# Folding the last square of each norm's sum into TensorE, and five reordered steps, in a two-block network on one core

## The chip, the core and the metric

The kernel runs on one core of a Trainium2 chip. A core has a matrix engine (TensorE, PE in the profile, with its weight loads as PEld), VectorE (DVE), ScalarE (ACT), GpSimd (POOL) and SyncE (SP), which here only starts transfers. The engines run their own instruction lists in order and meet only through semaphores. The metric is the device time of one execution in microseconds. Three executions of the kernel before took 1575.3, 1575.3 and 1575.46 us, median 1575.3.

## What is computed

Two network blocks follow one another on 512 tokens of 1024 features, everything in float32. In short:

```python
# first block
shift, scale, gate = split(silu(c) @ ada_w[0] + ada_b[0], 3)
h = rmsnorm(x, norm_g[0]) * (1 + scale) + shift
x = x + gate * mamba2_mixer(h)      # in-projection, conv, chunked state space scan,
                                    # y * silu(z), rms over each of 4 groups of 512, out-projection
kv = (rmsnorm(x, kv_norm_g) * (1 + kv_scale) + kv_shift) @ kv_w
x = x + gate1 * stick_breaking_mixer(rmsnorm(x, norm_g[1]) * (1 + scale1) + shift1, kv)
x = rmsnorm(x, final_g)
# second block
z = rmsnorm(x, norm_mix_g) @ w_in          # then an HGRN2 mixer and a banded attention
x = x + merged @ w_out
h2 = rmsnorm(x, norm_ffn_g); x = x + (silu(h2 @ w_gate) * (h2 @ w_up)) @ w_down
x = x + sigmoid(rmsnorm(x, norm_ple_g) @ w_ple_gate) * (p @ w_ple_proj)
```

Each `rmsnorm` needs the mean of the squares over the 1024 features of a token (over 512 in the mamba mixer's groups). The features lie on partitions, in 8 (or 4) tiles of 128, so the sum of squares is a sum over tiles and then over partitions.

## The kernel before

**Layout.** `X[:, k, :]` holds feature tile k of the residual stream for all 512 tokens. A projection is a row of output blocks of 128 features, each accumulated in one of three PSUM banks over the feature tiles k. float32 is reached by splitting: ScalarE rounds an operand to a high part, VectorE subtracts it to get the low part, and TensorE adds three products in the reduced float format (L646 high x high, L647, L648). The weights come in chunks of 128 x 2048 words through two buffers: SyncE loads `raw`, ScalarE makes `whi` (L1857, function `high`), VectorE makes `wlo` (L1162, function `rest`). The helper `behind(kind, n)` puts one such conversion, that of the chunk after the one of block (kind, n), at the place in an engine's list where it is called.

**Order.** There is no scheduler. Each engine's list is written by hand in one function, and `weave` mixes two or three generators by fixed counts of steps: where a generator yields decides what stands between its pieces on that engine. `Once` leaves out waits that an earlier one already covers.

**Sums of squares.** ScalarE squares tile after tile into `SQ` or one of three `T` tiles (L1877). An adder sums them in `SQ` (or `R`): VectorE for the first norm (L1183), GpSimd for all others (L2430). When the last add is done (`s_sqa`), TensorE multiplies the 128 x 128 matrix `ones` by that tile as true float32 (L690, function `sum_of`), which leaves the sum over partitions in all partitions of a bank. ScalarE turns it into 1/sqrt in `R` (L1864, L1865). There are ten such sums: `x`, `y0` to `y3` (four squares each), `out`, two for `so` (accumulated in `R` and `SQ`), `wo` and `fd`.

**The places around the change.**
- Start: `sum_of("x")` stands after the second of eight groups of small matmuls that make the first `ada` vector; ScalarE's copies for those groups (L1917) stand behind its 1/sqrt.
- After block cv 1 of the in-projection, VectorE copies the two transposed `dt` tables out of PSUM (L1349, L1350), and TensorE uses them (L789) four feature steps later.
- The scan (`ssd`): unit u = 4g + c is chunk c of group g, written in four pieces. On VectorE piece 2 ends with the state update (L1311, L1316), piece 3 makes `XD` and `XW` (L1321, L1327) and, for c = 0, the four gated products of the previous group (L1333). On TensorE `sum_of` of the previous group stands at the head of piece 2 of c = 2. The last group's pieces are woven into the out-projection (`out_proj`, a piece every two or three of its steps).
- kv: TensorE first makes the eight blocks `pp` of an unrelated product (L824 to L826), with `sum_of("out")` among them. ScalarE copies each to `PO` (L2084) and makes the eight high parts of the kv input (L1890); VectorE makes `T` (L1112) and the low parts (L1116). Then come the kv projections, the first two blocks together (`both`: 8 feature steps of 6 matmuls).
- sb: the same pattern once more for the query projection, whose first two blocks stand behind the kv blocks.

## Time and profile before

| | |
|---|---|
| median of 3 executions | 1575.3 us |
| profiled execution, its own time | 1575.3 us |
| its span, first to last instruction | 1573.5 us |
| TensorE busy | 1539.8 us, 98% of the span |
| VectorE, ScalarE, GpSimd busy | 954.1, 678.2, 114.2 us |
| mean granted clock of TensorE | 0.992 |
| float32 sums over partitions (L690) | 20 records, two for each of 10 |
| GpSimd adds (L2430) | 47 |

Busy time of TensorE includes the tail of each pipelined matmul, so a gap shows as idle only beyond that tail. The number behind the arrow in brackets names what ended an idle stretch. The first 12.9 us of TensorE are a wait for the first weights. Rows of several engines in one fence below are in order of time.

### The profile page before, as it was taken

What the parts mean: (1) busy time and instruction counts of PE and PEld (TensorE: products, weight loads), DVE (VectorE), ACT (ScalarE), POOL (GpSimd) and SP (SyncE); (2) the same over time, 40 slices, a digit from 0 to 9 for tenths busy, and PEclk for the clock granted to TensorE, in tenths of its full rate; (3) what the DMA queues carried; (4) which work ended last, traced back from release to release, by engine and by line L of the source; (5) the groups of instructions that cost most, each with busy time, mean ns of one, the idle gap of its engine ahead of it and who ended that gap; (6) DMA issues with size and microseconds to landing.
All of it is one profiled execution on the core that took longest, in us unless ns stands there. A gap on an engine that the chain in (4) does not pass through costs nothing. (4 is left out here: it accounts for less than half of the span.)

```text
span 1573.5 us, 19600 instructions
## 1 busy us (share of the span) xinstructions
PE 1539.8 (98%) x7978; PEld 1230.4 (78%) x7978; DVE 954.1 (61%) x1201; ACT 678.2 (43%) x958; POOL 114.2 (7%) x78
## 2 busy tenths in 40 slices
PE   5999999989999999999999999999999999999998
PEld 3788887868889766678898886678888888888877
DVE  4769798997882756765358536654544444332445
ACT  4556576764432555654222355533342322231232
POOL 0000000123300000014000000000120000000110
PEclk7999999999999999999999999999999999999999
DMA  7434344424592210113211122122222222222233
GB/s 324 163 134 154 132 147 143 148 69 173 215 369 112 81 54 27 54 55 110 93 69 54 54 81 94 68 77 84 83 105 98 90 107 82 105 101 101 76 111 120
DMA packets 47384, 177.74 MB, mean 113 GB/s; under 512 B 3616, under 2 KB 20512, under 8 KB 31680
## 3 DMA queue, kind: packets, MB, share of 16 engines
q1 hardware_dynamic: 30368, 167.44, 28.6%
q10 hardware_dynamic: 16928, 9.06, 2.2%
q8 instruction: 63, 1.03, 0.3%
q14 instruction: 25, 0.20, 0.0%
HBM read 172.23 MB, written 4.26 MB: 112 GB/s over the span
## 5 line engine op out<-in xcount | busy, mean ns | idle before, releaser
L646 PE MATMUL bank<-HH,whi 128*128 128x512 f32 x1352 | 554.4, 410 | 2.0 <-issue 1.6
L648 PE MATMUL bank<-HH,wlo 128*128 128x512 f32 x1352 | 528.5, 391 | 0.0
L647 PE MATMUL bank<-HL,whi 128*128 128x512 f32 x1352 | 528.2, 391 | 0.0
L1162 DVE TENSOR_TENSOR wlo<-raw,whi 128x2048 fp32r<-128x2048 f32 (+2 forms) x118 | 267.4, 2266 | 111.7 <-ACT whi L1857 110.4
L646 PEld LDWEIGHTS bank<-HH,whi 128*128 128x128 f32 x1352 | 254.6, 188 | 79.3 <-issue 33.0
L648 PEld LDWEIGHTS bank<-HH,wlo 128*128 128x128 f32 x1352 | 254.4, 188 | 54.7
L647 PEld LDWEIGHTS bank<-HL,whi 128*128 128x128 f32 x1352 | 255.0, 189 | 47.8 <-issue 3.1
L1857 ACT ACTIVATE whi<-raw 128x2048 fp32r<-128x2048 f32 (+2 forms) x118 | 222.4, 1884 | 102.9 <-PE bank L648 102.8
L2430 POOL TENSOR_TENSOR SR<-SR,tmp 128x512 f32<-128x512 f32 x35 | 61.6, 1761 | 592.9 <-ACT tmp L1877 591.9
L678 PE MATMUL bank<-whi,HH 128*128 128x256 f32 x256 | 74.3, 290 | 0.0
L679 PE MATMUL bank<-whi,HL 128*128 128x256 f32 x256 | 72.4, 283 | 0.0
L680 PE MATMUL bank<-wlo,HH 128*128 128x256 f32 x256 | 72.4, 283 | 0.0
L1481 DVE TENSOR_TENSOR_SCAN W<-W,cc 128x511 f32<-128x511 f32 (+3 forms) x64 | 49.0, 808 | 34.6 <-ACT W L2163 34.5
L648 PE MATMUL bank<-FH,wlo 128*128 128x512 f32 x176 | 68.5, 389 | 0.0
L647 PE MATMUL bank<-FL,whi 128*128 128x512 f32 x176 | 68.5, 389 | 0.0
L646 PE MATMUL bank<-FH,whi 128*128 128x512 f32 x176 | 68.5, 389 | 0.0
L1788 DVE TENSOR_TENSOR pst<-bank,SR 128x512 f32<-128x512 f32 x22 | 15.1, 692 | 72.0 <-PE bank L648 72.0
L1800 DVE SCALAR_TENSOR_TENSOR tmp<-tmp,bank 128x512 f32<-128x512 f32 x22 | 15.1, 688 | 65.0 <-PE bank L648 65.0
L2399 ACT ACTIVATE FH<-tmp 128x512 fp32r<-128x512 f32 x22 | 13.9, 632 | 85.9 <-DVE tmp L1800 85.9
L679 PEld LDWEIGHTS bank<-whi,HL 128*128 128x128 f32 x256 | 49.1, 192 | 1.0 <-issue 1.0
L678 PEld LDWEIGHTS bank<-whi,HH 128*128 128x128 f32 x256 | 49.1, 192 | 1.0 <-issue 1.0
L2395 ACT ACTIVATE tmp<-pst 128x512 f32<-128x512 f32 x22 | 13.9, 632 | 82.4 <-DVE pst L1788 82.4
(310 smaller groups left out, 2139.9 us busy)
## 6 DMA issues: line engine op xcount, KB each, us to landing
raw<-wstream SPq DMA_DIRECT2D x113, 1024.0 KB, 4.8
aslot<-tstream SPq DMA_DIRECT2D x24, 512.0 KB, 3.3
A<-astream SPq DMA_DIRECT2D x8, 1024.0 KB, 18.3
AC<-scratch ACTq DMA_DIRECT2D x16, 512.0 KB, 5.2
QT<-tstream SPq DMA_DIRECT2D x12, 512.0 KB, 5.8
OZ<-tstream SPq DMA_DIRECT2D x12, 512.0 KB, 7.3
raw<-wstream SPq DMA_DIRECT2D x4, 768.0 KB, 4.3
X<-xT SPq DMA_DIRECT2D x1, 2048.0 KB, 8.3
```

The costliest lines, as they stand in the source:

```text
L646: e.matmul(o, wh[:, k, c], hi[:, kb0 + k, :], start=first and k == 0, stop=False)
L647: e.matmul(o, wh[:, k, c], lo[:, kb0 + k, :], start=False, stop=False)
L648: x = e.matmul(o, wl[:, k, c], hi[:, kb0 + k, :], start=False, stop=last and k == kb - 1)
L678: e.matmul(o, HH[:, k, ts], wh[:, k, :], start=(k == 0), stop=False)
L679: e.matmul(o, HL[:, k, ts], wh[:, k, :], start=False, stop=False)
L680: x = e.matmul(o, HH[:, k, ts], wl[:, k, :], start=False, stop=(k == 7))
L1162: e.tensor_tensor(wlo[:, i % 2, 0:n], raw[:, i % 2, 0:n], whi[:, i % 2, 0:n].bitcast(F32), ALU.subtract).then_inc(s_lo, 1)
L1481: x = e.tensor_tensor_scan(k, k, diag[:, last], 0.0, ALU.mult, ALU.add)
L1788: e.tensor_tensor(pstage[n % 3][:, :], bank_of("fg", n)[:, :], R, ALU.mult).then_inc(s_fgr, 1)
L1800: e.scalar_tensor_tensor(q, q, 0.5, bank_of("fu", n)[:, :], ALU.mult, ALU.mult).then_inc(s_fu, 1)
L1857: e.activation(whi[:, i % 2, 0:n], raw[:, i % 2, 0:n], ACT.Copy).then_inc(s_hi, 1)
L2430: e.tensor_tensor(acc, acc, tile, ALU.add).then_inc(s_sqa, 1)
```

## The change

- `sum_of` makes two float32 products with `ones` into the same bank: the accumulated tile, and the last square straight from its own tile. The last add of each sum goes away (one on VectorE, nine on GpSimd), so `s_sqa` counts less; the second product waits for `s_sq`.
- `sum_of` of y0 to y2 stands at the end of the scan's piece 1 on TensorE, not at the head of piece 2.
- VectorE's gated products (L1333) move from the end of the scan's piece 3 to the end of piece 2.
- VectorE's two copies of the `dt` tables come one step of the in-projection later.
- kv: `sum_of("out")` and its 1/sqrt come after two `pp` blocks, not four; ScalarE's eight high parts stand behind all eight copies to `PO`; the conversion of the second kv chunk stands behind the load of the sigmoid tables.
- sb: the conversion of the second query chunk comes after the fifth of eight feature tiles, on ScalarE (from after the seventh) and on VectorE (from after the eighth).

```diff
--- before.py
+++ after.py
@@ -186,7 +186,7 @@
 HH_AT, HL_AT = h_table()
 
 SQ_AT = {"x": 0, "y0": 8, "y1": 12, "y2": 16, "y3": 20, "out": 24, "so": 32, "wo": 48, "fd": 56}
-SA_AT = {"x": 0, "y0": 7, "y1": 10, "y2": 13, "y3": 16, "out": 19, "so": 26, "wo": 40, "fd": 47}
+SA_AT = {"x": 0, "y0": 6, "y1": 8, "y2": 10, "y3": 12, "out": 14, "so": 20, "wo": 32, "fd": 38}
 SUM_AT = {"x": 1, "y0": 2, "y1": 3, "y2": 4, "y3": 5, "out": 6, "so2": 7, "so": 8, "wo": 9, "fd": 10}
 
 
@@ -683,11 +683,13 @@
             if half == 1:
                 x.then_inc(s_blk, 1)
 
-        def sum_of(name, bank, acc=SQ, n=7):
+        def sum_of(name, bank, q, acc=SQ, sqa=None, sq=None):
 
             w.wait_ge(l_con, 16)
-            w.wait_ge(s_sqa, SA_AT[name] + n)
-            e.matmul(bank[:, :], ones, acc[:, :], start=True, stop=True).then_inc(s_sum, 1)
+            w.wait_ge(s_sqa, sqa or SA_AT[name] + {"y": 2}.get(name[0], 6))
+            e.matmul(bank[:, :], ones, acc[:, :], start=True, stop=False)
+            w.wait_ge(s_sq, sq or SQ_AT[name] + {"y": 4}.get(name[0], 8))
+            e.matmul(bank[:, :], ones, q, start=False, stop=True).then_inc(s_sum, 1)
 
 
         def fold(i):
@@ -708,7 +710,7 @@
                              A[i][:, 256 * k:256 * k + 256], start=(k < 4), stop=(k > 3))
             x.then_inc(s_mv, 1)
             if i == 1:
-                sum_of("x", aux[0])
+                sum_of("x", aux[0], T[0][:, :])
             if i > 0:
                 fold(i - 1)
         fold(7)
@@ -736,10 +738,10 @@
                         x = e.matmul(aux[3][:, 128 * q:128 * q + 128], flat(ST[:, 2 * q:2 * q + 2, :]),
                                      Cc[g % 2][:, 128 * c:128 * c + 128], start=True, stop=True)
                     x.then_inc(s_to, 1)
-                yield
                 if 0 < g < 4 and c == 2:
                     w.wait_ge(s_cb, min(g + 1, 4))
-                    sum_of(f"y{g - 1}", aux[1], n=3)
+                    sum_of(f"y{g - 1}", aux[1], R)
+                yield
                 if u < 15:
                     if cv_ == 0:
                         w.wait_ge(s_fin, 10 * gv + 1)
@@ -799,7 +801,7 @@
                 yield from blocks(chunk_of["out", 8 * g + n], [("out", 8 * g + n)], (n % 4,), 512,
                                   h_ready(f"out{g}"), HH, HL, 4 * (g % 2))
                 if g == 2 and n == 3:
-                    sum_of("y3", aux[1], n=3)
+                    sum_of("y3", aux[1], R)
                 yield
 
         weave((chain(out_proj(0), out_proj(1)), 66), (chunks, 28))
@@ -813,8 +815,8 @@
         i = chunk_of["pp", 0]
         wh, wl = (t[:, i % 2, :].rearrange("p (k n) -> p k n", k=2) for t in (whi, wlo))
         for n in range(8):
-            if n == 4:
-                sum_of("out", aux[0])
+            if n == 2:
+                sum_of("out", aux[0], T[0][:, :])
             o, c = aux[1 + n % 4][:, :], slice(128 * n, 128 * n + 128)
             w.wait_ge(s_hi, i + 1)
             w.wait_ge(s_lo, i + 1)
@@ -907,10 +909,10 @@
         first = both("hq", 0, "in2")
         run(take(first, 3))
         w.wait_ge(s_bk, 32)
-        sum_of("so", aux[1], R, 13)
+        sum_of("so", aux[1], T[0][:, :], R, SA_AT["so"] + 11, SQ_AT["so"] + 15)
         run(first)
         run(block("hq", 2, "in2"))
-        sum_of("so", aux[0], SQ, 14)
+        sum_of("so", aux[0], T[1][:, :], SQ, SA_AT["so"] + 12, SQ_AT["so"] + 16)
         w.wait_ge(s_rr, SUM_AT["so2"])
         w.wait_ge(s_go, 8)
         for t in range(4):
@@ -1063,7 +1065,7 @@
         first = both("fg", 0, "ffn")
         run(take(first, 3))
         w.wait_ge(s_bs, 16)
-        sum_of("wo", aux[0])
+        sum_of("wo", aux[0], T[0][:, :])
         run(first)
         for i11 in range(11):
             if i11 > 0:
@@ -1085,7 +1087,7 @@
 
         first = both("pg", 0, "ple")
         run(take(first, 3))
-        sum_of("fd", aux[0])
+        sum_of("fd", aux[0], T[0][:, :])
         run(first)
         for n in range(2, 8):
             run(block("pg", n, "ple"))
@@ -1177,7 +1179,7 @@
         lg = vcol("lb")
         e.tensor_tensor(lbt[:, 0:4], lg, lg, ALU.subtract).then_inc(s_lb, 1)
 
-        for k in range(1, 8):
+        for k in range(1, 7):
             w.wait_ge(s_sq, k + 1)
             w.wait_ge(s_sqa, k - 1)
             e.tensor_tensor(SQ, SQ, T[(k - 1) % 3][:, :], ALU.add).then_inc(s_sqa, 1)
@@ -1314,6 +1316,12 @@
                                             EL[:, c, 8 * g:8 * g + 8].unsqueeze(2).to_broadcast([128, 8, 64]), ALU.mult))
                         w.wait_ge(s_ts, 3 * g + c + 1)
                         e.tensor_tensor(ST[:, :, :], ST[:, :, :], heads(aux[4][:, :]), ALU.add).then_inc(s_st, 1)
+                if g > 0 and c == 0:
+                    w.wait_ge(s_fin, 10 * g)
+                    for q in range(4):
+                        n = 4 * (g - 1) + q
+                        e.scalar_tensor_tensor(Y[:, n, :], XS[(g - 1) % 2][:, q, :], 0.5, Y[:, n, :],
+                                               ALU.mult, ALU.mult).then_inc(s_y, 1)
                 yield
                 if u < 15:
                     hs, xd = slice(8 * gv, 8 * gv + 8), XD[(u + 1) % 2]
@@ -1326,12 +1334,6 @@
                         w.wait_ge(s_ts, 3 * gv + cv_)
                         e.tensor_tensor(XW[:, :, :], xd[:, :, :], WE[:, cv_, hs].unsqueeze(2).to_broadcast([128, 8, 64]),
                                         ALU.mult).then_inc(s_xw, 1)
-                if g > 0 and c == 0:
-                    w.wait_ge(s_fin, 10 * g)
-                    for q in range(4):
-                        n = 4 * (g - 1) + q
-                        e.scalar_tensor_tensor(Y[:, n, :], XS[(g - 1) % 2][:, q, :], 0.5, Y[:, n, :],
-                                               ALU.mult, ALU.mult).then_inc(s_y, 1)
                 yield
                 if 0 < g < 4 and c == 2:
                     w.wait_ge(s_rr, SUM_AT[f"y{g - 1}"])
@@ -1343,12 +1345,12 @@
                 yield
 
         first, chunks = in_proj(0), ssd()
-        run(take(first, 15))
+        run(take(first, 16))
         bank = bank_of("tk", 0)
         w.wait_ge(s_blk, blk_done("tk", 0))
         e.tensor_copy(dtk[:, :, :], bank[:, 0:128].rearrange("p (c h) -> p c h", c=4))
         e.tensor_copy(atk[:, :, :], bank[:, 128:256].rearrange("p (c h) -> p c h", c=4)).then_inc(s_tk, 1)
-        run(take(first, 5))
+        run(take(first, 4))
         w.wait_ge(s_sel, 1)
         w.wait_ge(s_tk, 1)
         e.tensor_tensor(flat(WE[:, :, :]), bank[:, 256:352], flat(atk[:, 0:3, :]), ALU.subtract).then_inc(s_we, 1)
@@ -1436,7 +1438,8 @@
             low_shifted("sb", k, ada[:, 40:48])
             if k < 5:
                 normed("sb", k + 3, G1[:, 16:24])
-        behind("q", 0)
+            if k == 4:
+                behind("q", 0)
 
         def gate_att(n, src):
             if n < 7:
@@ -2076,22 +2079,19 @@
 
 
         for n in range(8):
-            if n == 4:
+            if n == 2:
                 w.wait_ge(s_sum, SUM_AT["out"])
                 w.wait_ge(s_res, 32)
                 rsqrt(aux[0][:, :], D, R[:, :]).then_inc(s_rr, 1)
             w.wait_ge(s_ppm, n + 1)
             e.activation(PO[:, n, :], aux[1 + n % 4][:, :], ACT.Copy).then_inc(s_pp, 1)
-            if n > 4:
-                high_shifted("kv", n - 5, ada[:, 24:32])
-
-
-        for k in range(3, 8):
+
+
+        for k in range(8):
             high_shifted("kv", k, ada[:, 24:32])
-        behind("k", 0)
         sigmoids()
         for n in range(8):
-            if n % 2 == 0 and n > 0:
+            if n % 2 == 0:
                 behind("k", n)
             w.wait_ge(s_blk, blk_done("k", n))
             e.activation(KT[:, n, :], bank_of("k", n)[:, :], ACT.Copy).then_inc(s_kt, 1)
@@ -2118,7 +2118,7 @@
             high_shifted("sb", k, ada[:, 40:48])
             if k == 2:
                 token_copy("v", 7, VT, s_vt)
-            if k == 6:
+            if k == 4:
                 behind("q", 0)
 
         def query(n):
@@ -2430,7 +2430,7 @@
             e.tensor_tensor(acc, acc, tile, ALU.add).then_inc(s_sqa, 1)
 
         def add_x(name, k):
-            if k > 0:
+            if 0 < k < 7:
                 add(SQ_AT[name] + k + 1, SA_AT[name] + k, T[(k - 1) % 3][:, :])
 
         def low(stage, k, src):
@@ -2447,8 +2447,6 @@
                 for n in range(4):
                     if g > 0 and c == 1 and n % 2 == 0:
                         add(SQ_AT[f"y{g - 1}"] + 2 + n // 2, SA_AT[f"y{g - 1}"] + 1 + n // 2, R)
-                    if g > 0 and c == 2 and n == 0:
-                        add(SQ_AT[f"y{g - 1}"] + 4, SA_AT[f"y{g - 1}"] + 3, R)
                     yield
 
         def out_split(g):
@@ -2475,7 +2473,7 @@
         weave((chain(out_proj(0), out_proj(1)), 66), (chunks, 28))
         run(chain(out_proj(2), out_proj(3)))
 
-        for n in range(1, 8):
+        for n in range(1, 7):
             for m, acc in ((2 * n - 2, R), (2 * n - 1, SQ)):
                 add(SQ_AT["so"] + m + 3, SA_AT["so"] + m + 1, T[m % 3][:, :], acc)
```

ScalarE's list where the kv input is made. `PO<-` are the copies of the `pp` blocks, `SR<-` the 1/sqrt, `HH<-` the high parts, `whi<-raw` a weight conversion. Before:

```order
L2084 ACTIVATE PO<-bank 128x512
L1864 ACTIVATE SR<-zz,eps 128x512
L1865 ACTIVATE SR<-SR 128x512
L2084 ACTIVATE PO<-zz 128x512
L2084 ACTIVATE PO<-tt 128x512
L1890 ACTIVATE HH<-tmp,ada 128x512
L2084 ACTIVATE PO<-tt 128x512
L1890 ACTIVATE HH<-tmp,ada 128x512
L2084 ACTIVATE PO<-bank 128x512
L1890 ACTIVATE HH<-tmp,ada 128x512 x6
L1857 ACTIVATE whi<-raw 128x2048
L1871 ACT_TABLE_LOAD
```

The same place now:

```order
L2087 ACTIVATE PO<-zz 128x512
L2087 ACTIVATE PO<-tt 128x512
L1867 ACTIVATE SR<-zz,eps 128x512
L1868 ACTIVATE SR<-SR 128x512
L2087 ACTIVATE PO<-tt 128x512
L2087 ACTIVATE PO<-bank 128x512
L2087 ACTIVATE PO<-zz 128x512
L2087 ACTIVATE PO<-tt 128x512 x2
L2087 ACTIVATE PO<-bank 128x512
L1893 ACTIVATE HH<-tmp,ada 128x512 x8
L1874 ACT_TABLE_LOAD
L1860 ACTIVATE whi<-raw 128x2048
```

The first high part has moved behind the last copy, and the table load ahead of the conversion.

VectorE's list at the query projection's input (`HL<-` low parts, `tmp<-X` the scaled tiles, `wlo<-raw` a weight conversion). Before:

```order
L1112 SCALAR_TENSOR_TENSOR tmp<-X,G,SR 128x512
L1116 SCALAR_TENSOR_TENSOR HL<-tmp,ada,HH 128x512
L1112 SCALAR_TENSOR_TENSOR tmp<-X,G,SR 128x512
L1116 SCALAR_TENSOR_TENSOR HL<-tmp,ada,HH 128x512 x3
L1162 TENSOR_TENSOR wlo<-raw,whi 128x2048
```

Now:

```order
L1114 SCALAR_TENSOR_TENSOR tmp<-X,G,SR 128x512
L1118 SCALAR_TENSOR_TENSOR HL<-tmp,ada,HH 128x512
L1114 SCALAR_TENSOR_TENSOR tmp<-X,G,SR 128x512
L1164 TENSOR_TENSOR wlo<-raw,whi 128x2048
L1118 SCALAR_TENSOR_TENSOR HL<-tmp,ada,HH 128x512 x3
```

The conversion stands ahead of the last three low parts.

VectorE's list at the `dt` tables (`dtk`, `atk` the copies, `tmp<-U` the convolution taps, `Bc` its gated result). Before:

```order
L1349 COPY dtk<-bank 128x128
L1350 COPY atk<-bank 128x128
L1235 SCALAR_TENSOR_TENSOR tmp<-U,cv,tmp 128x512
L1236 SCALAR_TENSOR_TENSOR tmp<-U,cv,tmp 128x512
L1237 SCALAR_TENSOR_TENSOR tmp<-U,cv,tmp 128x512
L1251 SCALAR_TENSOR_TENSOR Bc<-tmp 128x512
```

Now:

```order
L1237 SCALAR_TENSOR_TENSOR tmp<-U,cv,tmp 128x512
L1238 SCALAR_TENSOR_TENSOR tmp<-U,cv,tmp 128x512
L1239 SCALAR_TENSOR_TENSOR tmp<-U,cv,tmp 128x512
L1253 SCALAR_TENSOR_TENSOR Bc<-tmp 128x512
L1351 COPY dtk<-bank 128x128
L1352 COPY atk<-bank 128x128
```

The two copies have moved behind the taps of block cv 1 and the gate of block cv 0.

## Rows read from the trace of the kernel before

**Rows 1.** The page, part 1, busy time of TensorE:
```profile
PE 1539.8 (98%) x7978; PEld 1230.4 (78%) x7978; DVE 954.1 (61%) x1201; ACT 678.2 (43%) x958; POOL 114.2 (7%) x78
```

**Rows 2.** Chain of waits (start, us, what), around two adjacent float32 products:
```profile
872.39 0.23 PE bank L648
...
914.74 0.87 PE tt L971 x2
915.61 0.86 PE zz L964 x2
```

**Rows 3.** Windows (stretch, us, busy by engine, granted clock, DMA): the half clock:
```profile
22.60:43.10 20.50, 19.76 (x125) 12.21 (x118) 13.43 (x28) 9.36 (x16) 0.00 (x0) 0.50 0.63 253
...
333.20:336.70 3.50, 3.50 (x12) 2.71 (x11) 3.46 (x5) 1.79 (x7) 3.50 (x4) 0.51 0.94 364
```

**Rows 4.** Timeline (start, us, engine, line, what, idle before), first sum:
```profile
17.56 1.93 PE L690 MATMUL zz<-SR,cc 128*128 128x512 f32 x2 [0.29 <-DVE SR L1183]
...
19.60 0.69 ACT L1864 ACTIVATE SR<-zz,eps 128x512 f32<-128x512 f32 x1 [3.13 <-PE zz L690]
```

**Rows 5.** Timeline at the `dt` tables, VectorE and TensorE:
```profile
59.38 0.28 DVE L1350 COPY atk<-bank 128x128 f32<-128x128 f32 x1
...
61.94 0.38 PE L789 MATMUL bank<-atk,cc 128*128 128x128 f32 x2
...
62.12 0.68 DVE L1251 SCALAR_TENSOR_TENSOR Bc<-tmp 128x512 f32<-128x512 f32 x1
```

**Rows 6.** Timeline of the scan's last group, VectorE and TensorE:
```profile
318.10 2.49 DVE L1333 SCALAR_TENSOR_TENSOR Y<-XS,Y 128x512 f32<-128x512 f32 x4
...
332.79 1.64 PE L731 MATMUL bank<-XW,BT 128*128 128x512 f32 x2 [3.74 <-DVE XW L1327]
...
351.79 1.09 PE L764 MATMUL tt<-E,XD 128*64 128x128 f32 x16 [0.94 <-DVE E L1300]
```

**Rows 7.** Timeline of the kv input and its first two blocks, all engines:
```profile
421.54 0.63 ACT L1877 ACTIVATE tmp<-X 128x512 f32<-128x512 f32 x1 [2.21 <-DVE X L1374]
...
423.60 1.12 PE L690 MATMUL zz<-SR,cc 128*128 128x512 f32 x2 [0.24 <-POOL SR L2430]
...
428.06 0.71 ACT L1890 ACTIVATE HH<-tmp,ada 128x512 fp32r<-128x512 f32 x1
...
428.81 0.75 DVE L1116 SCALAR_TENSOR_TENSOR HL<-tmp,ada,HH 128x512 fp32r<-128x512 f32 x1
...
430.08 0.39 PE L646 MATMUL bank<-HH,whi 128*128 128x512 f32 x1
...
430.28 0.60 ACT L2084 ACTIVATE PO<-bank 128x512 f32<-128x512 f32 x1 [0.15 <-PE bank L826]
...
439.49 1.28 ACT L1871 ACT_TABLE_LOAD   x1
439.56 2.29 DVE L1162 TENSOR_TENSOR wlo<-raw,whi 128x2048 fp32r<-128x2048 f32 x1
...
440.79 1.08 ACT L2097 ACTIVATE KT<-bank 128x512 f32<-128x512 f32 x2
...
441.96 0.47 PE L646 MATMUL bank<-HH,whi 128*128 128x512 f32 x1 [0.83 <-issue]
```

**Rows 8.** Timeline of the query input, all engines:
```profile
525.82 0.75 DVE L1112 SCALAR_TENSOR_TENSOR tmp<-X,G,SR 128x512 f32<-128x512 f32 x1
525.85 1.91 ACT L1857 ACTIVATE whi<-raw 128x2048 fp32r<-128x2048 f32 x1
...
527.62 0.39 PE L646 MATMUL bank<-HH,whi 128*128 128x512 f32 x1
...
528.39 0.75 DVE L1116 SCALAR_TENSOR_TENSOR HL<-tmp,ada,HH 128x512 fp32r<-128x512 f32 x1 [0.50 <-ACT HH L1890]
```

**Rows 9.** Timeline of TensorE at the last sum, `fd`:
```profile
1527.17 0.39 PE L648 MATMUL bank<-HH,wlo 128*128 128x512 f32 x1
1528.16 1.13 PE L690 MATMUL zz<-SR,cc 128*128 128x512 f32 x2 [0.60 <-POOL SR L2430]
```

## The prediction

> **What bounds the kernel now.** The page's busy times come first: TensorE is busy 1539.8 of 1573.5 us, all other engines well below [rows 1]. So the question for every edit is what it adds to TensorE's list and what it makes TensorE wait for. The chain of waits gives the price of one product without waiting: a float32 product of 512 columns is two records and moves the list on by 0.86 to 0.87 us even when it stands behind another one, a product in the split format by 0.23 [rows 2]. The windows show where TensorE ran at its lower level, 1.2 instead of 2.4 GHz: about 20.5 us at the start, and 3.5 us right behind a wait of 3.7 us in the scan [rows 3, 6]. The timelines of the places that the change touches give the rest. What TensorE waits for the sums today is small: 0.3 us at x [rows 4], 0.4 at out (its list was free at 423.2, it began at 423.6) [rows 7], and at fd from 1527.40 (0.23 behind the last start) to 1528.16, 0.76 [rows 9]. The other seven sums are not waited for. That is 1.5 us to be won, against ten new products.
>
> **Part 1, ten more products.** With the clock up each costs 0.86 [rows 2].
> - x: the list is free about 17.27, so both products run from there. The present product took 1.93 with its tail [rows 4] against 1.12 at [rows 7], so it ran largely at 1.2 GHz; how much of the added one does no row tells, so it costs between 0.86 and 1.7. I take 1.1, minus the 0.3 of wait that goes: +0.8 (bounds 0.6 and 1.4). ScalarE's 1/sqrt at 19.60 and its copies behind it, for which TensorE waits next, shift by this.
> - y0, y1, y3: 0.86 each, +2.6. TensorE waits for none of them now, and the last square comes ahead of the add that goes.
> - y2: TensorE later idles 0.94 in front of the product at 351.79, waiting for VectorE [rows 6]. The added product falls into that gap as far as VectorE is not itself held up by TensorE's blocks. Bounds 0 and 0.86; I take +0.3.
> - so (two) +1.7, wo +0.9: nothing is waited for there before, so nothing comes back.
> - fd: 0.86 for the product, 0.76 of wait and about 0.1 of restart gone [rows 9]: 0.0. Both tiles lie ready when TensorE comes.
>
> Together +6.3; out is in part 4. No engine but TensorE is near the end-setting path at these sums, so an add less on GpSimd gives nothing.
>
> A rule that speaks against this price: the Trainium skill, "TensorE: Matmul & The Clock Gate", section "Back-to-back issue gap", gives about 131 ns a product of 512 columns in sustained streams; "FP8 and Floating Point Precision", section "TensorE Precision Notes", gives true float32 four passes. An estimate from the two pages is 0.52 us a sum, and the total would fall by about 3 us. The trace disagrees on both counts of time (0.23 and 0.86), so it is not used.
>
> **Part 2, the dt tables.** TensorE took them at 61.94 with the copies long done (59.66) [rows 5]. Now the copies stand behind the gate, which ends at 62.80; two copies of 0.28 that overlap a little end at 63.2. TensorE waits to 63.25: +1.3 (0.9 if the copies start closer, 1.6 if they are slower). Nothing else on TensorE hides it: the next matmuls stand behind L789 in its list.
>
> **Part 3, the gated products.** 2.49 us of VectorE work [rows 6] now stands ahead of XD and XW. In groups 0 and 1 VectorE idles there. In the last group it works without a gap up to XW of unit 14, for which TensorE waits 3.74 us until 332.79 [rows 6]. The products stood ahead of that XW before and do now, so this moment stays; what TensorE loses earlier on XW of unit 13, at most 2.5, comes out of the 3.74. 0.0 (bounds -0.5 and +1.0: the two VectorE orders meet GpSimd's adds differently).
>
> **Part 4, kv.** The last square is done at 422.17 [rows 7]. The sum now stands two blocks of 6 x 0.23 = 1.37 us earlier, at 420.5, before that square exists. TensorE waits to 422.2, makes it by 423.15, and the other six blocks (8.2) end at 431.35; before, kv began at 430.08. The last block's copy to PO starts 0.2 behind that [rows 7] and ends at 432.15. Only then comes the first high part: 432.05 instead of 428.06, 4.0 later. Its low part (VectorE, 428.81 before) ends at 433.55, and kv begins at 433.6, 3.5 later, after 2.25 us of waiting. From there VectorE and ScalarE make the parts as fast as before. The chunk for the third block stood right behind the eighth high part; now the table load of 1.28 us [rows 7] stands between. So its low part, 439.56 plus 2.29 before, is 4.0 + 1.3 = 5.3 later, and TensorE goes on at 447.2 instead of 441.96, having been ready at 433.6 + 48 x 0.228 = 444.55. Part 4 is +5.2, with the added product in it. What is gained, 1/sqrt about 0.9 us earlier, meets nobody: VectorE can only make the first tiles sooner. Bounds: +3.5 if the conversion gets in early, +6.
>
> A second rule would make it dearer: the Trainium skill, "ScalarE: Activation LUTs", section "What ACT_TABLE_LOAD costs", counts 1.38 us of drain beside the load, which would make part 4 +6.6 and the total 1591.4. Here ScalarE's next instruction starts 1.30 after the load began (439.49, 440.79) [rows 7], so I count 1.3.
>
> **Part 5, sb.** VectorE ended the eighth scaled tile at 526.57 [rows 8]. The conversion (2.29 [rows 7]) now follows at once; ScalarE's half of it stands two high parts earlier than at 525.85 and is ready. So the sixth low part ends at 526.5 + 2.3 + 0.7 = 529.5. TensorE reached its sixth feature step at 527.62 [rows 8]. It waits to 529.5, the last two parts keep ahead of it, and the conversion itself was not waited for before. +1.9 (if ScalarE's half is late, as late as 527.75, +3.1; if VectorE was ahead by then, +1.0).
>
> **Sum.** 6.3 + 1.3 + 0.0 + 5.2 + 1.9 = +14.7 us, on the profiled execution's own 1575.3 (span 1573.5), which is also the median shown: 1590.0 us. No term hides another, since each shifts the whole rest of the program.
>
> **The rivals.**
> - A, the clock falls in the new waits. A wait of 3.74 was followed by 3.5 us at half clock, which loses 1.7 [rows 3, 6]. The new ones are 2.25 and 2.7 us, twelve apart, and 1.9 at sb. Waits of 1 us (fd, L764) were followed by no fall. For it: they are long, and nearer to 3.74 than to 1. One fall gives 1591.7, two 1593.4. Chance 20%.
> - B, the moves are covered. If ScalarE and VectorE had enough lead at kv, sb and the dt tables, only the ten products stay: 6.3 plus the 0.4 net at out, 1582.0. Against it: in each of the three places the rows give no lead, they are within 0.5 us of TensorE. Chance 9%.
> - C, the other side. The start runs 20.5 us at half clock behind a gap of ScalarE's making [rows 3, 4]. If the longer sum keeps TensorE active enough that the full clock holds, up to 10.2 us come back, and 1.7 more if the two shorter waits in the scan replace the one that cost a dip: 1590.0 - 11.9 = 1578.1, not slower within what can be told. It decides as soon as the clock holds in nearly all of 22.6 to 43.1. Against it: the gap that follows the sum is as long as before (ScalarE's two steps and a copy), and the small matmuls behind it kept the lower level for 20 us though TensorE was busy 19.8 of them. Chance 4%.
>
> **How the numbers follow.** Forecast 67%, A 20%, B 9%, C 4%. The likeliest is 1590.0. Its own spread from the bounds (parts 3, 4 and 5 mostly) is about 1587 to 1592.5. The range takes in A, and the upper part of the way to B: 1584 to 1594.5, leaving out B and C in full. What a measurement can tell from no change is 0.2%, 3.15 us. Faster only if C comes with more: 0.01; same 0.04; slower 0.95.
>
> **What would show it.** Twenty more records of the sum's line and 38 GpSimd adds. TensorE idle about 1.3 before L789's place, 2.2 before the first kv block, 2.7 before the third, 1.9 in the first query pair; no idle before the sum at fd, and the last product of each sum 0.86 behind the one before. The forecast is wrong if the kv blocks start less than 3 us later against the pp blocks, if the table load does not stand in front of that conversion in time, or if the granted clock differs in 22.6 to 43.1. If the wait at the last XW grows, part 3 is wrong.

## The result, and the profile after

The changed kernel takes 1589.5 us (median of 4 runs, 1585.44 to 1590.96), the kernel before beside it 1575.38 (1575.3 to 1576.75): a ratio of 1.0081, 95% interval 1.0065 to 1.0096. It is slower, by about the 14.7 us forecast. But the runs of the changed kernel lie 5.5 us apart and those of before 1.5, and the profiled execution of after is one of the short ones: 1586.5 us, span 1584.7. Its differences add up to 11.2 us, not 14. That is the first thing to explain.

Page, part 1, busy times, against [rows 1]: TensorE has its 20 records and 5.9 us more, GpSimd nine additions less.
```profile
PE 1545.7 (98%) x7998; PEld 1232.6 (78%) x7998; DVE 949.9 (60%) x1200; ACT 678.1 (43%) x958; POOL 99.8 (6%) x69
```
Windows of after (stretch, us, busy by engine, granted clock, DMA share, GB/s), against [rows 3]:
```profile
16.87:30.50 13.63, 9.38 (x104) 5.32 (x104) 6.09 (x16) 6.78 (x13) 0.00 (x0) 1.00 1.02 421
30.55:40.70 10.15, 9.48 (x49) 6.45 (x38) 7.98 (x15) 4.51 (x7) 0.00 (x0) 0.50 0.56 205
433.30:436.70 3.40, 3.40 (x9) 2.62 (x10) 3.40 (x6) 1.76 (x3) 0.00 (x0) 0.50 1.05 405
535.70:539.10 3.40, 3.40 (x10) 2.66 (x9) 0.00 (x0) 0.00 (x0) 0.00 (x0) 0.50 0.56 224
```
At the start, half clock (1.2 GHz) came only at 30.5 and lasted 10 us instead of 20.5. The half clock at 333 us in the scan is gone. Two new stretches stand behind two new waits, at kv and at sb. The start in the timeline (start, us, engine, line, what, idle before), against [rows 4]:
```profile
16.97 1.13 PE L690 MATMUL zz<-SR,cc 128*128 128x512 f32 x2
17.93 1.02 PE L692 MATMUL zz<-tmp,cc 128*128 128x512 f32 x2
20.73 0.61 PE L700 MATMUL zz<-sel,AP 128*128 128x1 f32 x4 [1.78 <-ACT AP L1920]
```
The first product took 1.13 where it took 1.93 before, so the clock was already up. The `dt` tables, against [rows 5]: VectorE copies at 59.70 and TensorE has idled 1.16.
```profile
59.70 0.28 DVE L1352 COPY atk<-bank 128x128 f32<-128x128 f32 x1
...
60.04 0.49 PE L791 MATMUL bank<-atk,cc 128*128 128x128 f32 x2 [1.16 <-DVE atk L1352]
```
The scan's last group, against [rows 6]: the gated products (Y) stand ahead of XD and XW, and TensorE's one wait of 3.74 has become one of 1.93 and one of 0.67.
```profile
316.01 2.49 DVE L1323 SCALAR_TENSOR_TENSOR Y<-XS,Y 128x512 f32<-128x512 f32 x4
...
320.98 1.13 PE L733 MATMUL bank<-XW,BT 128*128 128x512 f32 x2 [1.93 <-DVE XW L1335]
...
326.48 0.68 DVE L1315 TENSOR_TENSOR ST<-ST,EL 128x512 f32<-128x512 f32 x1
326.51 1.80 POOL L2430 TENSOR_TENSOR SR<-SR 128x512 f32<-128x512 f32 x1 [6.13 <-ACT SR L1880]
...
331.55 1.13 PE L733 MATMUL bank<-XW,BT 128*128 128x512 f32 x2 [0.67 <-DVE XW L1335]
...
349.51 1.09 PE L766 MATMUL tt<-E,XD 128*64 128x128 f32 x16 [0.68 <-DVE E L1302]
```
The kv input, against [rows 7]: the folded sum, the last copy to PO, the first high and low part, kv, the table load, the chunk of the third block, the third block.
```profile
420.46 1.12 PE L690 MATMUL zz<-SR,cc 128*128 128x512 f32 x2 [0.35 <-POOL SR L2430]
421.00 0.63 ACT L1880 ACTIVATE tmp<-X 128x512 f32<-128x512 f32 x1 [2.21 <-DVE X L1376]
421.68 1.12 PE L692 MATMUL zz<-tmp,cc 128*128 128x512 f32 x2
...
431.05 0.60 ACT L2087 ACTIVATE PO<-bank 128x512 f32<-128x512 f32 x1 [0.76 <-PE bank L828]
431.54 1.32 ACT L1893 ACTIVATE HH<-tmp,ada 128x512 fp32r<-128x512 f32 x2
...
433.18 0.67 PE L646 MATMUL bank<-HH,whi 128*128 128x512 f32 x1 [2.17 <-DVE HL L1118]
...
441.10 1.28 ACT L1874 ACT_TABLE_LOAD   x1
...
444.40 2.29 DVE L1164 TENSOR_TENSOR wlo<-raw,whi 128x2048 fp32r<-128x2048 f32 x1 [1.39 <-issue]
...
446.80 0.47 PE L646 MATMUL bank<-HH,whi 128*128 128x512 f32 x1 [0.88 <-issue]
```
The query input, against [rows 8]: the conversion ahead of the sixth low part, and TensorE's wait for that part.
```profile
531.32 2.29 DVE L1164 TENSOR_TENSOR wlo<-raw,whi 128x2048 fp32r<-128x2048 f32 x1
...
533.52 2.07 DVE L1118 SCALAR_TENSOR_TENSOR HL<-tmp,ada,HH 128x512 fp32r<-128x512 f32 x3
...
534.42 0.47 PE L646 MATMUL bank<-HH,whi 128*128 128x512 f32 x1 [1.80 <-DVE HL L1118]
```
The last sum, against [rows 9]: no idle time in front of it, and two products 0.86 apart.
```profile
1538.31 0.40 PE L648 MATMUL bank<-HH,wlo 128*128 128x512 f32 x1
1538.55 1.02 PE L690 MATMUL zz<-SR,cc 128*128 128x512 f32 x2
1539.41 1.02 PE L692 MATMUL zz<-tmp,cc 128*128 128x512 f32 x2
```

To split the difference, the 5976 products in the split format ("dense" below) of two traces are laid side by side in order, and the growth of the lag of one behind the other is read at each place. "Folds alone" and "moves alone" are the first two experiments below.

| place | forecast | after | another trace |
|---|---|---|---|
| start, with the x sum | +0.8 | -3.2 | +1.2 (folds alone) |
| dt tables | +1.3 | +1.4 | +1.4 (moves alone) |
| y0, y1, y3 | +2.6 | +2.6 | +2.7 (folds alone) |
| y2 | +0.3 | -1.3, both | +0.4 (folds alone) |
| gated products | 0.0 | (in y2) | -1.7 (folds and scan, less y2) |
| out sum and kv | +5.2 | +5.4 | +8.3 (moves alone) |
| sb | +1.9 | +3.7 | +2.1 (moves alone) |
| so, wo, fd | +1.7, +0.9, 0.0 | +1.7, +0.9, +0.1 | +1.7, +0.9, 0.0 (folds alone) |
| elsewhere | 0.0 | -0.1 | |
| sum | +14.7 | +11.2 | |

### The profile page after: what moved, and what is told of

Read it like the earlier page. It is cut to its first block and busy times, and to the rows that moved or that the text cites. A ratio compares the mean times of both kernels' runs of the same rounds, so it can differ in the third digit from the quotient of the medians.

```text
span 1584.7 us, 19616 instructions
## 1 busy us (share of the span) xinstructions
PE 1545.7 (98%) x7998; PEld 1232.6 (78%) x7998; DVE 949.9 (60%) x1200; ACT 678.1 (43%) x958; POOL 99.8 (6%) x69
## 5 line engine op out<-in xcount | busy, mean ns | idle before, releaser
L2430 POOL TENSOR_TENSOR SR<-SR,tmp 128x512 f32<-128x512 f32 x30 | 54.9, 1830 | 604.8 <-ACT tmp L1880 603.9
```

The lines of the kernel that those rows point to most:

```text
L2430: e.tensor_tensor(acc, acc, tile, ALU.add).then_inc(s_sqa, 1)
```

## The experiments

All are edits of the kernel before unless said otherwise, timed beside it on one chip. "Clock" is the mean granted clock that each run lists.

**Folds alone.** Every sum takes the last square in a second product; no move.
```diff
-            e.matmul(bank[:, :], ones, acc[:, :], start=True, stop=True).then_inc(s_sum, 1)
+            e.matmul(bank[:, :], ones, acc[:, :], start=True, stop=False)
+            w.wait_ge(s_sq, ...)
+            e.matmul(bank[:, :], ones, q, start=False, stop=True).then_inc(s_sum, 1)
```


> Only the sums are changed: the last square goes straight into a second product on TensorE, and every move in the instruction order is left out. By the sum of the prediction (theory S) this part alone costs 6.3 us: x 0.8, y0, y1 and y3 0.86 each, y2 0.3, so 1.7, wo 0.9, fd 0.0; so 1581.6 us, with the sum at L690 taking two products of 0.86 each where x, wo and so stand on a path on which TensorE is the last to be ready. The rival R reads the trace after: the first product of the dense part there came 3.2 us earlier than before, because GpSimd has one addition fewer in front of it and full clock lasted to 30.5 us instead of 22.7; if that gain belongs to the folded x sum, it is here too, and the sum is 6.3 - 0.8 - 3.6 = 1.9 us, so 1577.2 us. If the gain is only when the chip lowers the clock in one run or another, the start of this kernel reads full clock up to some 22 us as before and the time is that of S.

Measured: 1579.17 us (8 runs), ratio 1.0024 (1.0013 to 1.0034). The eight fall in two groups: 1577.25 to 1577.67 at clock 0.995, and 1580.67 to 1582.81 at 0.991 to 0.992. The upper group is 4.9 to 7.0 us over the 1575.8 of before beside it, which holds the forecast for the folds with the 0.4 us net at out, 6.7; its trace adds up to 7.3. The lower group is 4 to 5 us less. So both theories were half right: the start has ways of its own, and a run takes one or the other.

**Moves alone.** All moves; one product a sum and the last addition on GpSimd or VectorE, as before.
```diff
-            if n == 4:
+            if n == 2:
                 sum_of("out", aux[0])
```
(and likewise the other moves of the change, without its sums.)


> Every move in the order is made, and the sums stay as they were (one product each, with the last addition on GpSimd or VectorE). Theory S: dt tables 1.3, gated products 0.0, kv 5.2 less the added product 0.86 = 4.3, sb 1.9, together 7.5 us, so 1582.8 us. Rival A (the clock falls behind the new waits) adds 1.65 us at sb, where the trace after shows half clock for 3.4 us behind a wait of 2.0 us: 1584.5 us. What the trace after shows of the scan (1.4 us less than before in its last group) gives, if it belongs to the moved gated products and not to the folded sums, 1.7 us less: 1581 to 1583 us.

Measured: 1590.85 us (4 runs, 1588.4 to 1591.69), ratio 1.0092 (1.0077 to 1.0108), 15 us against 7.5 expected: all three expectations missed. It is as slow as the whole change, so the folds cost nothing on top of the moves. The next two show why.

**The scan's moves alone.** y sums one piece earlier on TensorE, gated products one step earlier on VectorE.
```diff
-                yield
                 if 0 < g < 4 and c == 2:
                     w.wait_ge(s_cb, min(g + 1, 4))
                     sum_of(f"y{g - 1}", aux[1], n=3)
+                yield
```


> Only the scan's two moves are made: the gated products stand one step earlier on VectorE and the y sums one piece earlier on TensorE; sums as before. Theory S: 0.0 us, 1575.4 us. Rival M (the moved products change which wait comes last before L731, and the wait is short enough that the clock does not fall at 333 us): -1.5 to -2.5 us, 1573 to 1574 us, with no half clock between 333 and 337 us. A third, since the y sums without the fold need three additions on GpSimd: TensorE waits for the third one where it did not, by at most one addition, 1.7 us for each of three sums, so up to 1580 us.

Measured: 1578.56 us (11 runs), ratio 1.0021 (1.0012 to 1.0029): the third expectation. Timeline of TensorE in this kernel:
```profile
321.27 1.12 PE L731 MATMUL bank<-XW,BT 128*128 128x512 f32 x2 [1.93 <-DVE XW L1333]
331.84 1.13 PE L731 MATMUL bank<-XW,BT 128*128 128x512 f32 x2 [0.68 <-DVE XW L1333]
336.83 1.52 PE L690 MATMUL zz<-SR,cc 128*128 128x512 f32 x2 [2.97 <-POOL SR L2430]
```
The split wait of after is here too, so it comes from the gated products. But the y2 sum now idles 2.97 us for GpSimd's third addition, which the fold takes away.

**The moves ahead of kv alone.**
```diff
-            if n > 4:
-                high_shifted("kv", n - 5, ada[:, 24:32])
-        for k in range(3, 8):
+        for k in range(8):
             high_shifted("kv", k, ada[:, 24:32])
-        behind("k", 0)
         sigmoids()
         for n in range(8):
-            if n % 2 == 0 and n > 0:
+            if n % 2 == 0:
                 behind("k", n)
```
(and the out sum at block 2, above.)


> Only the moves ahead of kv are made: the out sum and its rsqrt at block 2, the high parts behind all the copies, the first conversion behind the table load. Sums as before. Theory S: 5.2 us less the product of 0.86 us that the fold would add, 4.3 us, so 1579.7 us, with the waits ahead of kv (2.25 us) and ahead of its third block (2.7 us). Rival A, as the trace after shows it: the first wait is 2.2 us, half clock follows for 3.4 us and costs 1.64 us, and the wait ahead of the third block is only 1.05 us; the sum is 4.4 us, which is the same time by other terms. The two are told apart by the granted clock between 430 and 437 us. A third: the out sum at block 2 waits for the seventh addition on GpSimd, since nothing is folded, which would add up to 1.7 us: 1581.4 us.

Measured: 1583.22 us (5 runs), ratio 1.0046 (1.0033 to 1.0058), +7.4; again the third expectation, only dearer. Timeline, GpSimd and TensorE:
```profile
422.44 1.27 POOL L2427 TENSOR_TENSOR SR<-SR,tmp 128x512 f32<-128x512 f32 x1 [1.29 <-ACT tmp L1877]
```
```profile
423.76 2.07 PE L690 MATMUL zz<-SR,cc 128*128 128x512 f32 x2 [2.91 <-POOL SR L2427]
```
TensorE waits 2.91 us for the seventh addition, and the clock is halved from 423.57, as that wait ends. In after, the fold starts at 420.46 and its second product needs only the square. The forecast of +5.2 was right because it had the fold under it.

**The x sum folded alone** (the edit of the first experiment, for x only).


> Of the ten folded sums only the first (x) is folded; all else as before. Theory S (a product costs its length): +0.8 us in every run, 1576.2 us. Theory W (the start has two ways, and the folded x sum opens the second): some runs show +0.8 to +1.2 us (1576 to 1577), and others some 4.2 us less than that (1572 us), as the runs with only the folds did, which stood at 1577.3 to 1577.7 with a mean granted clock of 0.995 and at 1580.7 to 1582.8 with 0.991 to 0.992. If the second way belongs to something else of the change, no run is under 1574 us.

Measured: 1575.38 us (11 runs), ratio 0.9997 (0.9988 to 1.0006). Eight runs lie from 1575.17 to 1576.43 (clock 0.990 to 0.993), three from 1572.09 to 1572.76 (0.995). The folded x sum opens the shorter way by itself, as theory W said, in fewer than half of the runs. Of the 77 runs of before in the four batches of comparisons two were under 1574 (1572.67 and 1573.32).

**Two products that do no work, behind the x sum.**
```diff
                 sum_of("x", aux[0])
+                for _ in range(2):
+                    e.matmul(aux[4][:, :], ones, SQ[:, :], start=True, stop=True)
```


> The kernel before, with two more float32 products of the same length right behind the x sum, into a PSUM bank that nobody reads; they do no work that is used. TensorE idles 1.78 us there before (19.49 to 21.27), so at full clock both (2 x 0.86) fit in the idle time. Theory W: the start's half clock comes of that idle stretch, so part of the 20.5 us at half clock goes and the dense part starts some 3 us earlier: 1572 us. Theory S: the clock falls as before, the two products run partly at half clock and reach over the end of the gap by up to 1.7 us: 1575.4 to 1577 us.

Measured: 1572.36 us (10 runs, 1571.45 to 1573.91), ratio 0.9981 (0.9972 to 0.9990): faster than both kernels by adding work. Timeline and windows of this kernel:
```profile
17.38 1.10 PE L690 MATMUL zz<-SR,cc 128*128 128x512 f32 x2 [0.50 <-DVE SR L1185]
18.32 1.88 PE L713 MATMUL bank<-SR,cc 128*128 128x512 f32 x4
20.26 0.61 PE L698 MATMUL zz<-sel,AP 128*128 128x1 f32 x4
```
```profile
16.60:30.20 13.60, 10.10 (x104) 5.50 (x100) 7.06 (x19) 6.78 (x13) 0.00 (x0) 1.00 1.02 420
30.25:40.40 10.15, 9.41 (x52) 6.40 (x45) 7.46 (x15) 3.92 (x7) 0.00 (x0) 0.50 0.47 187
```
The pair fills the 1.78 us in which TensorE idled, and full clock (2.4 GHz) lasts to 30.2 instead of 22.7. The dense part starts at 37.03 instead of 39.54. TensorE is now ahead of the stream of `A`, and the half clock of 30.2 stands at a wait for the next piece of it:
```profile
29.95 1.31 PE L707 MATMUL tt<-A,cact 128*32 128x256 f32 x12 [2.94 <-DMA A<-astream]
```
After has the same wait, 2.48 us until 29.96. By the Trainium skill, "TensorE: Matmul & The Clock Gate", section "What's actually happening", the throttled level is the default and activity releases it; these rows agree.

**ScalarE's high parts behind all copies, alone** (the second hunk above).


> Of the moves ahead of kv only one: ScalarE's high parts stand behind all eight copies instead of between the last three. The out sum stays at block 4 and the first conversion ahead of the table load. Theory S, from the working of part 4: the copy of the last block ends about 2.1 us after kv began before (430.08), the first high part comes at about 430.8 instead of 428.06, so kv starts about 2.3 us later (a wait of 2.3 us on TensorE), the third block 2.7 later than before: +2.7 us, 1578.1 us. Rival A: half clock for 3.4 us behind that wait, which costs up to 1.7 us: if the third block's weights are late anyway the dip is hidden in that wait (+2.7 still), else up to +4.4, 1579.8 us.

Measured: 1577.92 us (11 runs), ratio 1.0017 (1.0008 to 1.0026), +2.6 against 2.7. TensorE:
```profile
432.83 0.47 PE L646 MATMUL bank<-HH,whi 128*128 128x512 f32 x1 [2.17 <-DVE HL L1116]
```
Half clock followed from 434.15. Laid beside before, it cost 1.7 us, of which 1.1 came back at the third block, whose chunk is ready no sooner.

**The conversion behind the table load, alone** (the third hunk).


> Only ScalarE's half of the conversion for the third kv block is moved behind the table load and the sigmoids. High parts, sums and copies as before. Theory S: that half comes 1.3 us later (the table load, 1.28 us), TensorE was kept waiting for it hardly at all before (its list was ready within 0.3 us of 441.96), so +1.3 us, 1576.7 us. Rival: the sigmoids come ahead of it too and their own time counts, up to +2 us. Second rival: VectorE's low part of the conversion (439.56, 2.29 us) is what TensorE waits for, and it does not need ScalarE's half at once, so 0.0 us, 1575.4 us.

Measured: 1577.83 us (11 runs), ratio 1.0011 (1.0003 to 1.0020). The two medians lie 2.5 apart, the interval holds 0.5 to 3.2, and theory S said 1.3. The five runs at a clock of 0.992 have a median of 1576.35, 1.3 over the 1575.0 of before's runs at 0.991 to 0.994, which is theory S. In the trace, of a run at 0.999, the growth there is 1.4 us, and half clock followed for 1.6 more:
```profile
444.47 0.57 PE L646 MATMUL bank<-HH,whi 128*128 128x512 f32 x1 [2.26 <-issue]
```

**The dt tables and sb, alone.**
```diff
-        run(take(first, 15))
+        run(take(first, 16))
...
-        behind("q", 0)
+            if k == 4:
+                behind("q", 0)
```


> Two moves alone, far apart: the copies of the dt tables one block step later on VectorE, and the conversion for the first query pair earlier at sb on VectorE and ScalarE. Sums as before. Theory S: 1.3 us at the dt tables plus 1.9 us at sb, 3.2 us, 1578.5 us. Rival A: half clock for 3.4 us behind the wait at sb, 1.65 us more, as the trace after shows it (it is missing in the trace of the kernel with all moves and no folds, so it may come in some runs and not in others): 1580.2 us in those. Rival B (moves covered): 1575.4 us.

Measured: 1579.45 us (7 runs), ratio 1.0026 (1.0016 to 1.0037), 2.5 to 5.8 us for 3.2 expected. The trace grows by 1.4 at the tables and 2.0 at sb, with 0.7 more in the scan, where its half clock lasts 6.8 us (333.2 to 340.0), twice as long as before. Nothing follows at sb:
```profile
531.55 0.47 PE L646 MATMUL bank<-HH,whi 128*128 128x512 f32 x1 [1.80 <-DVE HL L1116]
```
```profile
529.40:540.00 10.60, 8.80 (x38) 6.21 (x37) 3.42 (x6) 3.98 (x5) 0.00 (x0) 1.00 0.29 100
```
The same 1.80 us of idle time as in after, and full clock behind it. The dip of after at sb is a matter of the run, not of the move.

**Folds and the scan's moves.**


> All folds and the scan's two moves; no other move. Theory S: 6.3 us and 0.0, 1581.6 us in runs whose start is as in the profile before, some 4 us less in those whose start kept the clock longer. The folds alone measured 1577.3 to 1577.7 in the latter and 1580.7 to 1582.8 in the former; the scan's two moves alone cost 2.7 us. Theory I (the moved y sums were dear without the fold only because TensorE waited for GpSimd's third addition, and folding takes that addition away): this kernel stands within 1 us of the folds alone, or up to 2 us below, since the trace after shows 1.4 us less in the last group. Theory N (the cost of the moves has nothing to do with the sums): 2.7 us above the folds alone, 1580.1 and 1584.4 us.

Measured: 1580.74 us (6 runs), ratio 1.0033 (1.0021 to 1.0045). Five runs at clock 0.992 or 0.993 are at 1580.33 to 1581.11 (folds alone 1580.67 to 1582.81) and one at 0.995 is at 1577.44 (1577.25 to 1577.67): theory I. In the folded kernel the moves cost nothing or win up to 1 us; without the folds they cost 2.7. TensorE at the y2 sum does not wait:
```profile
336.67 1.02 PE L690 MATMUL zz<-SR,cc 128*128 128x512 f32 x2
337.53 1.02 PE L692 MATMUL zz<-SR,cc 128*128 128x512 f32 x2
```
The last group, y2's product included, comes out 1.3 us shorter than before, as in after.

**Eight products that do no work.** The two above, and these:
```diff
+            if i == 6:
+                w.wait_ge(s_rr, 1)
+                for _ in range(3):
+                    e.matmul(aux[0][:, :], ones, SQ[:, :], start=True, stop=True)
...
+                    if u == 14:
+                        w.wait_ge(s_st, 3 * g + c)
+                        for _ in range(3):
+                            e.matmul(aux[4][:, :], ones, cc[:, 0:512], start=True, stop=True)
```


> The kernel before with eight float32 products of 0.86 us that nobody uses, all in TensorE's idle time: two behind the x sum (as in the run that measured 1572.4 us), three ahead of the seventh matvec of the start, where TensorE idles 2.94 us once the first two are there, and three ahead of the product that waits for the scan's unit 14, where it idles 3.6 us and half clock for 3.4 us follows. Theory W (the idle stretches are why the clock is halved): at the start 2 to 4 us more than the 3.0 us that the first two give, in the scan 1.6 us, 1568 us together (1567 to 1570). Theory S (idle time on TensorE's list is the only loss, the clock falls anyway): each filler costs what of it reaches over its gap, 1572 to 1575 us, and half clock stands at 30 to 40 us and at 330 to 334 us as before.

Measured: 1572.32 us (11 runs, 1570.88 to 1573.32), ratio 0.9982 (0.9973 to 0.9991): no better than two. The clock did as theory W says:
```profile
19.20:36.20 17.00, 15.16 (x139) 8.22 (x137) 9.73 (x21) 8.88 (x17) 0.00 (x0) 1.00 0.83 341
...
330.00:334.00 4.00, 3.04 (x18) 2.34 (x17) 3.96 (x5) 2.08 (x7) 3.87 (x4) 1.00 0.92 365
```
But the dense part starts at 36.62, only 0.4 earlier than with two: TensorE now idles 1.5 us there for other engines. In the scan VectorE is the one that comes last. The conversion kernel above shows it without any filler: the same long wait as before, by chance no half clock behind it, VectorE busy 9.90 of 10 us,
```profile
333.88 1.12 PE L731 MATMUL bank<-XW,BT 128*128 128x512 f32 x2 [3.67 <-DVE XW L1327]
```
```profile
330.00:340.00 10.00, 5.36 (x24) 3.46 (x24) 9.90 (x13) 7.17 (x15) 7.62 (x5) 1.00 0.65 210
```
and at the end of the group its lag behind before is the same as ahead of it (1.1 and 1.2 us). TensorE gains 1.7 us and waits them out in front of the next steps. Where another engine comes last, a clock that is up for these 3.4 us brings nothing. (The trace with eight products does gain 0.9 us in this group, but so do two traces without a filler there; the reason is given below, under the gated products.)

**The changed kernel with the two products behind its x sum.**


> The changed kernel with two more float32 products right behind its x sum, of which nothing is used, as in the run on the kernel before. Theory W (the spread of the changed kernel, 1585.4 to 1591.0 us, is the start's clock, and the two products keep it up): nearly all runs stand at 1585 to 1587 us, the median at 1586 us, 3 to 4 us under the 1589.5 us measured without them. Theory S (the spread comes from elsewhere, or the folded sum already does all that such products can do): the spread stays and the median is 1589.5 us or up to 1.7 us more.

Measured: 1585.21 us (5 runs, 1584.78 to 1585.72), ratio to before 1.0060 (1.0046 to 1.0074). The spread of 5.5 us is down to 0.9, at the lower end of what the changed kernel showed. Theory W holds: that spread was the start.

## Why the prediction was right

**The time.** 1590.0 was forecast, 1589.5 measured, in a range of 1584 to 1594.5. It is less exact than it looks. The thirteen runs known of the changed kernel go with the clock: six at 0.989 to 0.991 stand at 1589.8 to 1591.0, four at 0.992 to 0.994 at 1586.5 to 1588.8, three at 0.996 to 0.997 at 1585.4 to 1586.2. The median of all thirteen is 1588.8, 13.4 over before. The forecast holds for the first six, whose start, by their clock, is like that of the profile before; none of the six was traced. An estimate from the table, with the start of the folds alone (+1.2) in place of after's -3.2, is 1590.9 with the half clock at sb and 1589.3 without it, which brackets most of them. So the mechanism was right in most terms, and that 1590.0 and 1589.5 lie so close is in part luck: apart from the start, after has two errors of opposite sign, -1.6 in the scan and +1.8 at sb. By one of the prediction's own signs ("if the granted clock differs in 22.6 to 43.1") the forecast did not hold for the profiled execution, where it was 0.75 there and not 0.50.

**Ten more products.** The price of 0.86 [rows 2] came out: 0.89 each for y0, y1 and y3, and 0.4 for y2 in the trace of the folds alone. fd came out at 0.0 there and 0.1 in after: two products for one product and a wait, as worked out. x was mis-sized: +1.2 and +1.4 in two traces of the slower way (0.8 was taken, with bounds of 0.6 and 1.4), and -3.2 in after. Rival C named that mechanism and its place and gave it 4%. Against it stood that the idle time behind the sum is as long as before. It is, 1.78 us, and in after the clock stayed up all the same. Two things differ: the clock rose at 16.9 us (19.3 before), which nothing in the change moves, and TensorE had a product more ahead of the gap. Most traces at hand fit both being needed: folded but risen at 18.7 and 18.9 (folds alone; folds and the scan's moves), it fell within 3.5 us; risen at 16.5 but not folded (the scan's moves alone), it fell at 19.9; folded or filled and risen at 16.3 to 18.3 (x alone, two products, and the changed kernel with two), it held to 30 or 32 us. One does not fit: the kernel with eight products rose at 19.2 and held to 36.2, so with two products behind the sum, where the fold has one, the early rise was not needed. That is a pattern in a few traces, and why it is so was not tested.

**The dt tables.** Wait and growth as forecast (1.3; 1.4 measured).

**The gated products.** Forecast 0.0 (bounds -0.5 and +1.0), measured -1.7 with the folds. This is the step that failed: it had the products ahead of the same XW either way, "so this moment stays". The wait did split as foreseen, 1.93 and 0.67, but the moment itself came 1.2 us earlier, and VectorE's chain sets the pace of this group, so that came through. The clock that did not fall is not the reason; by the conversion kernel these 3.4 us are worth nothing here (a half clock of twice that length, in the kernel with the dt and sb moves, cost 0.7), so the 1.7 us that the prediction read out of [rows 3] for this dip was never to be had. Most of the earlier moment has a cause in the rows of before, VectorE and GpSimd:
```profile
326.84 1.70 DVE L1313 TENSOR_TENSOR ST<-ST,EL 128x512 f32<-128x512 f32 x1
```
```profile
326.72 1.28 POOL L2430 TENSOR_TENSOR SR<-SR 128x512 f32<-128x512 f32 x1 [4.72 <-ACT SR L1877]
```
GpSimd's addition began 0.12 us ahead, and VectorE's step took 1.70. In after VectorE began first (326.48 against 326.51): its step took 0.68, and the addition 1.80 instead of 1.28. Whoever comes second pays. The Trainium skill, "SBUF — State Buffer", section "Who interferes with whom", has a VectorE instruction with two SBUF inputs contend with a GpSimd instruction that reads SBUF, and has the order of issue, not the shape, decide who blocks; these four rows agree. The prediction named this meeting as a bound and did not look at who came first.

How much of the -1.7 belongs to the move is open, for the same meeting can turn without it. The kernel with ScalarE's high parts moved has the scan as before, and there VectorE came first:
```profile
328.17 0.67 DVE L1313 TENSOR_TENSOR ST<-ST,EL 128x512 f32<-128x512 f32 x1
328.35 1.64 POOL L2428 TENSOR_TENSOR SR<-SR 128x512 f32<-128x512 f32 x1 [5.03 <-ACT SR L1877]
```
Its wait for the last XW is 2.83 us instead of 3.74, and its last group 0.9 us shorter. So it is in three of the nine traces with the old order in the scan, and in all five with the new one, by margins of 0.03 to 0.28 us. Some 0.9 us of the -1.7 is thus this meeting, and 0.8 is left for the order itself (an estimate by subtraction). That part has two sides. VectorE's conversion ahead of the meeting takes 2.28 (after, 321.51) where it took 2.98 next to another addition of GpSimd (before, 321.17), and that is so in all traces of either order; the XW ahead of it takes 1.13 instead of 0.69 in turn. Against it, at the end of the group the moved products stand ahead of the next conversion, and TensorE comes to its chunk too early:
```profile
357.86 2.97 DVE L1164 TENSOR_TENSOR wlo<-raw,whi 128x2048 fp32r<-128x2048 f32 x1
360.94 0.47 PE L646 MATMUL bank<-HH,whi 128*128 128x512 f32 x1 [0.57 <-issue]
```
All five traces with the new order lose 0.8 to 0.9 us here, which the prediction did not see; the -1.7 is what is left after it.

**kv.** After is 0.5 us ahead of before when it comes here; with that taken off, the chain was right link by link (measured in brackets): first high part at 432.05 (432.1), wait of 2.25 (2.17), kv 3.5 later (3.6), third block 5.3 later (5.4). Only the sum itself began at 421.0 for 420.5, having waited 0.35 for GpSimd. ScalarE's conversion began 1.29 us after the table load did (441.10), as counted. The last wait came otherwise. Instead of 2.7 us, TensorE waited 0.88, since half clock had used up the rest. Rival A's price of 1.7 was nothing here, because the next wait was there to take it.

**sb.** Forecast 1.9 for the wait; it was 1.80 us of idle time and 2.0 to 2.1 of lag. In after half clock followed, 1.65 us more, with no wait behind it to hide it. This is rival A with one fall (20%); three other traces have the same wait and no fall.

**What the sum hid.** Against the before timed beside them, folds alone are 6.3 us by the median of their upper group and moves alone 15; both together are 14.7 by the six runs with the slower start. The additions on GpSimd that the folds take away are what the moved sums would wait for. The forecast was of both at once and so never needed this split; my own expectations for the parts did, and missed.

## What to carry to other kernels

A sum that is moved ahead needs its last operand earlier; ask which engine makes that operand before judging the move, and judge a group of edits together, since one may pay for another. An idle stretch of TensorE costs itself and also what the clock loses behind it, and that second part is only lost if TensorE sets the pace there and no later wait covers it. Filling such a stretch with a product of the same length is a two-line test, and here it was the only edit that gained: 3 us (0.19%) in the kernel before, and some 4 us in the changed one. Six more such products in two later idle stretches added nothing. And two engines that meet within a few tenths of a microsecond can turn a term of the sum by 0.9 us in a kernel whose edit is somewhere else; look at such a meeting in more than one trace before giving it to the edit.

## What the runs showed of the hardware

- **The start has more than one way for one program.** Before's runs list a clock of 0.990 to 0.994 or of 0.998 to 1.000, the second about 1 us longer: in a trace of that sort (the conversion kernel) there is no clock record before 45 us, the view then prints 1.00, and the durations show the lower level all along, as this row does, 1.93 where full clock gives 1.07 (after, at 21.27):
```profile
22.18 1.93 PE L707 MATMUL tt<-A,cact 128*32 128x256 f32 x16
```
  So a mean clock near 1 is not by itself a faster run.
- **Behind waits of about 2 us the clock falls in some runs and not in others.** At sb, 1.80 us of idle time was followed by half clock in one trace of four (after). In the scan, 1.93 was followed by it in two of five (moves alone, after with two products; not in after), 2.8 in none of two, and 3.6 to 3.8 in all but one (before [rows 6]; not in the conversion kernel, 3.67). At kv, 2.17 was followed by it in all five. So a dip is a chance that differs from place to place, not a term of the sum, and its price is what no later wait takes up: 0 of 1.7 in the scan, 0 at kv in after, 1.65 at sb in after.
